# Gathering the experts' rows in two passes, the first one during the last two experts, and summing four of nine tiles on TensorE

## The reference

```
h = h + HierMoE(rmsnorm(h))   # top-1 of 4 groups, then top-2 of its 8 SwiGLU experts: 32 experts in all
y = rmsnorm_final(h)
```

## Time and profile before

| | |
|---|---|
| median of 3 executions | 1834.32 us (1832.26 to 1834.6) |
| profiled execution, its own time | 1836.69 us |
| its span | 1834.9 us |
| PE busy | 1757.5 us, 96% of the span |
| DVE busy | 1052.8 us, 57% |
| ACT busy | 866.8 us, 47% |
| POOL busy | 105.6 us, 6% |
| mean granted TensorE clock | 0.98 |

### The profile page before, as it was taken

The page is one execution under the profiler, slowest core; times in us unless marked ns, Lnnn a source line. Parts: engine busy times, 40 slices in busy tenths (PEclk is TensorE's granted clock), DMA queues, the critical chain, the costliest instruction groups (busy, mean ns, idle before and its releaser), DMA issues. The chain is left out here.

```text
span 1834.9 us, 25589 instructions
## 1 busy us (share of the span) xinstructions
PE 1757.5 (96%) x10354; PEld 1561.3 (85%) x10354; DVE 1052.8 (57%) x1283; ACT 866.8 (47%) x1122; POOL 105.6 (6%) x130
## 2 busy tenths in 40 slices
PE   8999999999999999999999999989999999999980
PEld 7887887989898899999999988878888888888870
DVE  5346664533354432132333155568899998898967
ACT  4225554332443331121122133257888878888753
POOL 0010000000000010000000000011100000000003
PEclk9999999999999999999999999989999999999995
DMA  5231111002022222122221142189999999999958
GB/s 189 81 106 41 30 30 48 24 24 74 24 67 78 56 73 82 63 86 69 75 90 54 48 183 70 52 305 397 413 415 416 415 414 416 412 413 415 414 224 303
DMA packets 139321, 329.85 MB, mean 180 GB/s; under 512 B 13674, under 2 KB 91334, under 8 KB 114501
## 3 DMA queue, kind: packets, MB, share of 16 engines
q1 hardware_dynamic: 123556, 272.69, 40.1%
q0 software_dynamic: 10896, 38.74, 5.5%
q10 hardware_dynamic: 4752, 16.78, 2.2%
HBM read 286.08 MB, written 39.87 MB: 178 GB/s over the span
## 5 line engine op out<-in xcount | busy, mean ns | idle before, releaser
L2498 DVE TENSOR_TENSOR low<-raw,hig 128x2048 fp32r<-128x2048 f32 x192 | 431.2, 2283 | 57.9 <-ACT hig L2233 57.7
L2233 ACT ACTIVATE hig<-raw 128x2048 fp32r<-128x2048 f32 x192 | 359.5, 1915 | 22.8 <-ACT ye L2306 14.4
L2061 PE MATMUL bank<-hig,xel 128*128 128x512 f32 x512 | 202.7, 396 | 0.0
L2063 PE MATMUL bank<-hig,xeh 128*128 128x512 f32 x512 | 199.9, 390 | 0.0
L2062 PE MATMUL bank<-low,xeh 128*128 128x512 f32 x512 | 199.3, 389 | 0.0
L70 PE MATMUL bank<-xhi,glo 128*128 128x384 f32 (+1 forms) x552 | 180.0, 326 | 1.9 <-PEq L65 1.9
L72 PE MATMUL bank<-xhi,ghi 128*128 128x384 f32 (+1 forms) x552 | 180.0, 326 | 0.0
L71 PE MATMUL bank<-xlo,ghi 128*128 128x384 f32 (+1 forms) x552 | 179.9, 326 | 0.0
L70 PE MATMUL gproj<-xhi,glo 128*128 128x384 f32 (+1 forms) x384 | 131.7, 343 | 0.0
L71 PE MATMUL gproj<-xlo,ghi 128*128 128x384 f32 (+1 forms) x384 | 126.9, 330 | 0.0
L72 PE MATMUL gproj<-xhi,ghi 128*128 128x384 f32 (+1 forms) x384 | 126.8, 330 | 0.0
(11 more groups left out here) (426 smaller groups left out, 3561.1 us busy)
## 6 DMA issues: line engine op xcount, KB each, us to landing
raw<-in_w_e_gate_dram SPq DMA_DIRECT2D x64, 1024.0 KB, 7.9
raw<-in_w_e_up_dram SPq DMA_DIRECT2D x64, 1024.0 KB, 8.2
raw<-in_w_e_down_dram SPq DMA_DIRECT2D x64, 1024.0 KB, 7.6
graw<-in_w_in_dram SPq DMA_DIRECT2D x39, 512.0 KB, 3.8
expert_rows<-ye ACTq DMA_DIRECT2D x31, 512.0 KB, 8.3
xt<-in_x_prompt_dram SPq DMA_DIRECT2D x16, 512.0 KB, 3.7
expert_rows<-nil POOLq DMA_DIRECT2D x16, 512.0 KB, 4.0
braw<-in_w_branch_dram SPq DMA_DIRECT2D x24, 256.0 KB, 2.9
```

Of the source, the lines that this page charges most:

```text
L2061: nc.tensor.matmul(bank[:, :], xel[n % 2][:, kk, :], wh[:, k, :], start=(kk == 0), stop=False)
L2063: last = nc.tensor.matmul(bank[:, :], xeh[n % 2][:, kk, :], wh[:, k, :], start=False, stop=(kk == KC - 1))
L2233: nc.scalar.activation(hig[q % HI][:, :], raw[q % RAW][:, :], ACT.Copy).then_inc(high, 1)
L2498: nc.vector.tensor_tensor(low[q % RAW][:, :], raw[q % RAW][:, :], hig[q % HI][:, :].bitcast(F32), ALU.subtract).then_inc(lowed, 1)
```

## The change

In words:
- After its last gather for an expert, POOL waits in the expert stage until the stores of experts 0 to 29 have landed (s0 and s1 at 16*15), and then issues 18 gathers, two for each tile, bounded to the rows of `ysd` below LATE = 30*128. An index beyond the bound is left out. They write to buffers of the expert stage that are free by then; each waits on `used` for its buffer.
- In the last stage, POOL issues 18 further gathers to the same tiles with a second index list, `lidx`, in which every index below LATE is moved up by 2^20 and so is beyond the bound: these bring the rows of experts 30 and 31 alone. Before each pair it waits for the first pair of the tile.
- `lidx` is made in `slots`: a comparison with a product, an add and two copies more.
- TensorE sums tiles 1, 3, 5 and 7: for each half of 512 columns three float32 matmuls, identity by h, diag(w0) by a, diag(w1) by b, into one of four 1024-column PSUM tensors. DVE builds the eight diagonals (128x128) at the stage's start, and adds only tiles 0, 2, 4, 6 and 8. ACT and `scale` read the sum of those four tiles from PSUM. On DVE scale(t) now stands two places behind add(t).
- Buffers of the last stage and of `further` move.

```diff
+    lidx = [at("lidx", [P, NT], I32, CON + 1024 + 64 * k) for k in range(2)]
...
+    LATE = (NE - 2) * P
+    spent = lambda kind, n, h: place[kind, n, h] + 1
+    rows_at = [(e0, 0), (e0 + 4096, 0), (e0 + 8192, spent("u", NE - 2, 1)), (e0 + 16384, spent("u", NE - 2, 1))]
+    for kind, h in (("g", 0), ("g", 1), ("u", 0), ("u", 1)):
+        q = place[kind, NE - 1, h]
+        rows_at += [(raw_at[q % RAW] + 4096 * i, q + 1) for i in range(2)]
+        if kind == "u":
+            rows_at += [(hig_at[q % HI] + 4096 * i, q + 1) for i in range(2)]
+    rows_at += [(e0 + 12288, spent("u", NE - 1, 1)), (e0 + 20480, spent("u", NE - 1, 1))]
...
             pool.wait_ge(xturned, 2 * NE)
+            pool.wait_ge(found, 1)
+            pool.wait_ge(s0, 16 * (NE // 2 - 1))
+            pool.wait_ge(s1, 16 * (NE // 2 - 1))
+            for t in range(NT):
+                r = rows_of(t)
+                for k, dst in enumerate((ya, yb)):
+                    pool.wait_ge(used, rows_at[2 * t + k][1])
+                    pool.indirect_dma_start(dst[t][0:r, :], None, ysd[0:LATE, :],
+                                            bass.IndirectOffsetOnAxis(ap=sidx[k][0:r, t:t + 1], axis=0),
+                                            bounds_check=LATE - 1, oob_is_err=False).then_inc(ys_[t], 16)
...
+                nc.vector.tensor_scalar(isov[:, :, :], eid[:, :, :], float(LATE), float(1 << 20), ALU.is_lt, ALU.mult)
+                ve.drain()
+                nc.vector.tensor_tensor(isov[:, :, :], isov[:, :, :], eid[:, :, :], ALU.add)
...
             for t in range(NT):
                 r = rows_of(t)
+                pool.wait_ge(ys_[t], 32)
                 for k, dst in enumerate((ya, yb)):
                     pool.indirect_dma_start(dst[t][0:r, :], None, ysd,
-                                            bass.IndirectOffsetOnAxis(ap=sidx[k][0:r, t:t + 1], axis=0)).then_inc(ys_[t], 16)
+                                            bass.IndirectOffsetOnAxis(ap=lidx[k][0:r, t:t + 1], axis=0),
+                                            bounds_check=SLOTS - 1, oob_is_err=False).then_inc(ys_[t], 16)
+
+        @block.tensor
+        def _(pe):
+            pe.wait_ge(diagonal, 1)
+            for j, t in enumerate(ON_PE):
+                for half in range(2):
+                    out, c = banks[j][:, 512 * half:512 * half + 512], slice(512 * half, 512 * half + 512)
+                    if half == 0:
+                        pe.wait_ge(ys_[t], 64)
+                    nc.tensor.matmul(wide(out), ident[:, :], hrow(t, P)[:, 4 * half:4 * half + 4, :], start=True, stop=False)
+                    nc.tensor.matmul(out, dg[:, 2 * j, :], ya[t][:, c], start=False, stop=False)
+                    last = nc.tensor.matmul(out, dg[:, 2 * j + 1, :], yb[t][:, c], start=False, stop=True)
+                last.then_inc(added, 1)
...
+            for j, t in enumerate(ON_PE):
+                for k in range(2):
+                    last = nc.vector.tensor_scalar(dg[:, 2 * j + k, :], ident[:, :], wts[:, t, k:k + 1], None, ALU.mult)
+            last.then_inc(diagonal, 1)
             ve.wait_ge(g_in, 16)
-            for t in range(NT + 1):
-                if t < NT:
+            for t in range(NT + 2):
+                if t < NT and t not in ON_PE:
                     add(t)
-                if t >= 1:
-                    scale(t - 1)
+                if t >= 2:
+                    scale(t - 2)
```

More of the change, by code:

```diff
@@ L1620, in _ @@
                 memory_head(h)
-    psum = [top.enter_context(nc.psum_tensor(f"bank{i}", [P, 512], F32)) for i in range(8)]
-    PA, PB, TB, Z0, Z1, A0, A1, OB = psum
+    banks = [top.enter_context(nc.psum_tensor(f"banks{i}", [P, 1024], F32)) for i in range(4)]
+    PA, PB, TB, Z0, Z1, A0, A1, OB = [banks[i // 2][:, 512 * (i % 2):512 * (i % 2) + 512] for i in range(8)]
     mixT = at("mixT", [P, KC, T], F32, R2)
@@ L1745, in build @@
     wux = at("wux", [P, KC, DE], F32, 16384)
[L1746 to L1751, removed]
+    wdx = at("wdx", [P, 4, D], F32, OS)
+    xex = at("xex", [P, D], F32, OS + 16384)
+    xtx = at("xtx", [P, KC, P], F32, OS + 20480)
+    glx = at("glx", [P, DE], F32, OS + 24576)
+    htx = at("htx", [P, 4, P], F32, OS + 26624)
+    yex = at("yex", [P, D], F32, OS + 28672)
+    LATE = (NE - 2) * P
[7 more added lines that the diff above has]
+    rows_at += [(e0 + 12288, spent("u", NE - 1, 1)), (e0 + 20480, spent("u", NE - 1, 1))]
+    assert len(rows_at) == 2 * NT
+    ya = [at("ya", [P, D], F32, rows_at[2 * t][0]) for t in range(NT)]
+    yb = [at("yb", [P, D], F32, rows_at[2 * t + 1][0]) for t in range(NT)]
+    ys_ = [nc.alloc_semaphore(name=f"rows_in{t}") for t in range(NT)]
     fours = lambda t: t[:, :].rearrange("p (k n) -> p k n", k=4)
@@ L2632, in slots @@
                 ve.drain()
+                nc.vector.tensor_scalar(isov[:, :, :], eid[:, :, :], float(LATE), float(1 << 20), ALU.is_lt, ALU.mult)
+                ve.drain()
+                nc.vector.tensor_tensor(isov[:, :, :], isov[:, :, :], eid[:, :, :], ALU.add)
+                ve.drain()
                 for k in range(2):
-                    last = nc.vector.tensor_copy(sidx[k][:, :], eid[:, :, k])
+                    nc.vector.tensor_copy(sidx[k][:, :], eid[:, :, k])
+                    last = nc.vector.tensor_copy(lidx[k][:, :], isov[:, :, k])
                 last.then_inc(found, 1)
@@ L2667, in _ @@
             further(ve, body)
[L2672 to L2676, removed]
+    yo = [at("yo", [P, D], F32, 4096 * i if i < FULL else OS) for i in range(NT)]
+    gf = at("gf", [P, D], F32, OS + 4096)
+    junk = at("junk", [P, D], F32, OS + 8192)
+    ON_PE = [1, 3, 5, 7]
+    dg = at("dg", [P, 2 * len(ON_PE), P], F32, OS + 12288)
     with Stage(nc) as ctx:
-        g_in, summed, rooted, finished, stored, *ys_ = sems(
-            ctx, "z", "g_in summed rooted finished stored " + " ".join(f"y{t}" for t in range(NT)))
+        ctx.held += ys_
+        g_in, diagonal, summed, added, rooted, finished, stored = sems(
+            ctx, "z", "g_in diagonal summed added rooted finished stored")
         block = ctx.enter_context(nc.Block())
@@ L2705, in _ @@
                 R = slice(0, rows_of(t))
-                act.wait_ge(summed, t + 1)
-                nc.scalar.activation(junk[R, :], ya[t][R, :], ACT.Square, scale=D ** -0.5, accum_out=stat[R, t:t + 1])
+                if t in ON_PE:
+                    act.wait_ge(added, ON_PE.index(t) + 1)
+                    total = banks[ON_PE.index(t)]
+                else:
+                    act.wait_ge(summed, t + 1 - sum(u < t for u in ON_PE))
+                    total = ya[t]
+                nc.scalar.activation(junk[R, :], total[R, :], ACT.Square, scale=D ** -0.5, accum_out=stat[R, t:t + 1])
                 act.drain()
@@ L2716, in add @@
                 r = rows_of(t)
-                ve.wait_ge(ys_[t], 32)
+                ve.wait_ge(ys_[t], 64)
                 nc.vector.scalar_tensor_tensor(out=wide(ya[t][0:r, :]), in0=wide(ya[t][0:r, :]), scalar=wts[0:r, t, 0:1],
```

3 lines of the change are left out of this document (2 added, 1 removed).

## The result

The changed kernel takes 1846.67 us in the median of 4 runs (1845.41 to 1851.12), the kernel before 1833.29 of 4 (1832.08 to 1834.6): ratio 1.0073, 95% interval 1.0060 to 1.0085. That is 0.73% slower. The forecast was 1834.8 us, no measurable difference, with a range to 1845.0, so both were wrong. The profiled execution took 1845.41 us, with a span of 1843.7.

The account below looks back on a forecast made before the run. The prediction took DVE to bound the last stage before the change and TensorE's sums after it. Stage start +7.7 us and arithmetic -7.3 gave +0.4, so 1834.8 us, no measurable difference; range 1829.5 to 1845.

Parts of the forecast that it names:

- What bounds the kernel: Last stage before the change, 46.7 us: bound by DVE, with POOL's gathers only lead-in (8.1 us) or hidden.
- The early pass: POOL's 18 gathers ahead of the barrier: from 1769.8 us, at 1.25 us each after three dearer ones, ending at 1794.3 with waits.
- The last stage starts at S' = 1794.3 + 1.6: Barrier after the experts: waits for POOL's early issue, then 1.6 us; stage starts at 1795.9 us, 7.7 us later than before.
- The store of expert 31: Last expert store before the barrier: even with 7.7 us to landing it would land at 1792.3 us, ahead of POOL.
- The last stage: From its start: TensorE's sums become the chain, arithmetic ends after 35.5 us instead of 42.8, 7.3 us less; 3.96 us follow.
- The forecast's 29.8 for tile 8: DVE in the last stage: tile 8 summed at about 29.8 us after the stage's start.
- The forecast's path by TensorE and ACT: End of the last stage: TensorE finishes tile 7 at 30.6 us, ACT tile 8 at 34.2, DVE scales it until 35.5.
- Bounded gathers dearer to issue: Rival on POOL's gathers: 0.25 us more each gives 1840.5 us; decides from 0.14 us each; chance 0.31, shared with dearer waits and barrier.
- POOL is not held up beside the last stage's adds: Last stage: earlier gathers ran at 0.92 to 0.99 us beside DVE's adds, so the skill's contention rule isn't borne out there.
- TensorE at 1.2 GHz: Rival in the last stage: TensorE stays at low clock, arithmetic ends 18.5 us later, total 1853 us; chance 0.07.
- Faster: Rival: the early pass holds the barrier less long, 1830.6 us, or 1828 at a pace of 1.0 us; chance 0.17.
- the barrier at POOL dearer: Case at the barrier: waits and barrier at POOL cost more; no size given; chance 0.31 shared with dearer bounded gathers.

Follow-up runs that it names:

- one_block_alone: Last stage of the kernel before, without early pass, appended to the experts' block so no drain or barrier stands between; ratio 0.9991 to the kernel before.
- one_block: Changed kernel with the last stage appended to the experts' block, one semaphore replacing drain and barrier, same gathers; ratio 1.0028 to the kernel before.
- tensor_sum_one_block: Against the kernel before: no early pass, last stage in the experts' block, TensorE sums tiles 0, 2, 4, 6, identity times h first; ratio 0.9987.
- tensor_sum_alone: Changed kernel without the early pass: 18 whole gathers in the last stage, TensorE sums tiles 1, 3, 5, 7; ratio 1.0000 to the kernel before.
- two_passes_alone: Changed kernel with both gather passes but all nine tiles added on VectorE in the old order; ratio 1.0090 to the kernel before.
- whole_first_seven: Against the kernel before: one block, early pass for tiles 0 to 6, whole tiles 7 and 8 first, TensorE sums 0, 2, 4, 6; ratio 1.0007.

## Why the prediction was wrong

**What bounds the kernel** was half read. DVE did bound the last stage of before, but the rows were close behind. In the forecast that didn't matter, because late rows were to be small; it did in every experiment with whole rows.

**The early pass.** Its start was nearly right: POOL's waits were met at Z - 15.3 (forecast -14.8), and the first gather began 1.0 us later. Between the gathers the waits that were already met cost nothing (gaps of 0.30 us, as without them), where the forecast had 0.05 each. Its end was forecast at Z + 9.7 and came at 11.4. The first gather took 2.76 us and the second 1.87 beside DVE's subtraction, more than the bound of 2.16 for the first; the 16 others went at 1.30 instead of 1.25. Together 1.7 us, 14% of the error.

**The step that failed is "The last stage starts at S' = 1794.3 + 1.6".** I took the 1.6 us from a barrier that waited for ACT's store, and put it behind POOL's last issue. With gathers in flight the drain comes between. Issue's end to stage's start was 12.2 us: 8.3 to the landing of the last row, 2.5 more of the drain, 1.3 from there to the first instruction. That is 10.6 us of the 12.2 by which the span missed the forecast. The trace of before had it, in two rows of the sequencers that the prediction does not use: the last stage's own drain, and that of the experts' block.

```profile
L2677 POOLq DRAIN  x1: 25722/25722/25722, 1796.7 to 1796.7; - x1
```

```profile
L1754 POOLq DRAIN  x1: 3555/3555/3555, 1756.8 to 1756.8; - x1
```

The first ends at 1822.47, 11.3 us after POOL's last gather was issued (1811.12) and 0.8 after its rows had landed. It was hidden behind DVE. The second took 3.6 us with nothing in flight, hidden too. From these the stage's start would have come out at about Z + 22 (9.7 for the forecast issue, 11.3, 1.3), and the sign with it.

**The store of expert 31** was allowed 7.7 us among the gathers and took 8.4; hidden behind POOL, as written. Without the drain it is the next thing in the way, which the forecast did not say.

**The last stage** held in its sum: first late gather 0.78 us after the start (0.7), landing 2.9 us (3.5), first matmul at 7.8 (8.0), tile 1 summed some 7.3 us later (7.2), 5.15 us for each further tile (5.2), TensorE's end 30.7 (30.6), arithmetic 35.5 (35.5), tail 3.98 (3.96). The diagonals took 1.78 us (1.9). That the arithmetic came out at just 35.5 is in part luck: DVE's written order has the scaling of tile 5, for which it had to wait, ahead of tile 8's adds. The forecast's 29.8 for tile 8 leaves that out; it was summed at 31.9, and the end was DVE's own six instructions. The forecast's path by TensorE and ACT was 0.07 us from being the later one.

**The rivals.** Bounded gathers dearer to issue: by 0.05 us, under the 0.14 from which it decides. That POOL is not held up beside the last stage's adds, which the prediction read from the earlier trace rows, holds for before and for most gathers of after, but not for every run (see the last section). TensorE at 1.2 GHz: only at the start, as in the sum. Faster: no; the 1828 us named there for a pace of 1.0 doesn't follow from its rows (15 gathers at 0.25 us less are 3.75 us, from 1830.6 to 1826.9), and nothing hangs on it. The case that came, "the barrier at POOL dearer", had been put into one line of the chances with dear gathers, without a price of its own.

**Open.** What the 2.1 to 3.5 us after the last landing are (0.8 in the last stage's own block, 2.5 to 5.4 at the end of the kernels in one block whose landings can be read), and why a drain entered with nothing in flight costs 3.6 or 5.0, no run here separates. No run keeps the barrier and takes away the drain alone; that the barrier's part is small rests on one_block_alone. That the remaining 3.7 us of one_block are traffic rests on its landings and on the gain with fewer early gathers, which also left POOL free sooner; it is not shown.

## What to carry to other kernels

Before you put asynchronous transfers of an engine ahead of the end of a block, read the drain rows of that engine's queue: here a drain that ended 11.3 us after the last issue, hidden where it cost nothing, told what the same transfers would cost elsewhere (10.8 us). Where a stage is bound by arithmetic, look how far behind the arrival of its data is, since that is the most that relieving the engine can give. And rows fetched early are not free because the engines are busy elsewhere: here the one store on which the next stage waited landed 8.4 us after its issue, and 2.0 before.

## What the runs showed that was not expected

- A drain on POOL with indirect gathers outstanding: 23.8 us, to 2.5 us after the last landing; with nothing in flight 3.6 and 5.0 us. The other engines' drains at the same place in after took 0.07 us or less.
- A row that a bounded gather leaves out still is a packet. The queue's line for the whole last stage, first before (1788 to 1834 us), where the 18 gathers bring all their rows, then after (1804 to 1843.7 us), where they bring some 8 rows of 128 each:

```profile
q0 software_dynamic: 2464, 8.91, 52.9%
```

```profile
q0 software_dynamic: 2464, 0.58, 7.9%
```

  The number of packets is the same, 2464; what they carried fell from 8.91 to 0.58 MB. The late gathers landed 2.9 us after issue at the start, the whole ones of the earlier trace rows 5.6 at least. The issue costs 1.00 instead of 0.95 us.
- TensorE, at full clock, was granted it still after 1.6 us without work and not after 3.8 us (one record pair 1.12 against 2.07 us, tensor_sum_one_block). In tensor_sum_alone it lost it behind a gap of 2.41 us (pairs of 1.60 and 1.92 us).
- GpSimd beside VectorE: the first two gathers of after took 2.76 and 1.87 us beside the subtraction of weights, the other early ones 1.00. Beside the last stage's adds those of before took 0.92 to 0.99 and those of after 0.94 to 1.18, but single ones in other runs took far longer: three in two_passes_alone 2.0 to 2.1 us, one in one_block 1.96, one in whole_first_seven 3.32 (the fence). The Trainium skill (GPSIMD Engine Reference, 1. Specifications) names contention with VectorE's two-input instructions; the subtraction bears it out here, and so do these gathers, while most gathers beside adds show nothing of it.

```profile
1805.40 3.32 POOL L1815 DMA_INDIRECT ya<-expert_rows,lidx  x1 [0.30 <-issue]
```
